# Further blocks' lists in the second pair, the first x copied in halves, and the second gather inside the first down product

## The reference

```python
logits = x @ w_router + b_router          # 320 x 32
top_v, top_i = lax.top_k(logits, 4);  top_w = softmax(top_v)
# rows of x are grouped by expert in blocks, and for every block:
g = jnp.minimum(xb @ w_gate[e] + b_gate[e], 7.0)
u = jnp.clip(xb @ w_up[e] + b_up[e], -7.0, 7.0)
y = (g * sigmoid(1.702 * g) * (u + 1.0)) @ w_down[e] + b_down[e]
# y rows times top_w are summed back into their tokens; gated residual, final RMSNorm
```

## Time and profile before

| | |
|---|---|
| median of three runs | 1199.6 us |
| the profiled execution's own time | 1199.98 us |
| its span in the trace | 1198.0 us (2 us lie around it) |
| TensorE (PE) matmul busy | 1145.7 us, 96% |
| VectorE (DVE), ScalarE (ACT) busy | 300.2 us, 153.6 us |
| moved by DMA | 452.67 MB, mean 378 GB/s |
| mean granted TensorE clock | 0.982 |
| pairs of experts | from 253 us to 1185 us |

### The profile page before, as it was taken

How to read it: one execution, slowest core, us unless ns; L and a number is a source line. 1 busy time by engine, 2 the same in 40 slices (tenths; PEclk the granted TensorE clock), 3 DMA queues, 4 the chain that set the end, 5 groups by cost and what they waited for, 6 DMA issues and landing times.

```text
span 1198.0 us, 15518 instructions
## 1 busy us (share of the span) xinstructions
PE 1145.7 (96%) x6469; PEld 534.2 (45%) x6470; DVE 300.2 (25%) x667; ACT 153.6 (13%) x257; POOL 38.7 (3%) x50
## 2 busy tenths in 40 slices
PE   5999999999999999999999999999999999999995
PEld 2666547554353525252535353535353434444332
DVE  3243423623121212020303030302031212121143
ACT  1342240311010000000000010101010101011002
POOL 1021200400000000000000000000000000000000
PEclk9889999999999999999999999999999999999998
DMA  9573567659999999999999999999999999999992
GB/s 381 224 271 132 207 265 336 228 212 428 382 429 421 427 426 427 426 428 426 427 428 428 428 427 429 427 427 428 429 428 429 429 428 428 429 429 419 429 421 89
DMA packets 38788, 452.67 MB, mean 378 GB/s; under 512 B 4176, under 2 KB 6608, under 8 KB 7632
## 3 DMA queue, kind: packets, MB, share of 16 engines
q1 hardware_dynamic: 37984, 449.31, 89.5%
q0 software_dynamic: 752, 2.60, 0.6%
HBM read 447.99 MB, written 3.91 MB: 377 GB/s over the span
## 4 chain that ended last, share of the span: by engine, by line
PE 75%; DMA 19%; DVE 3%; ACT 2%; issue 1%; SPq 0%; DVEq 0%
PE ps L618 74%; DMA arena<-in_w_exp 18%; DVE arena L1382 2%; ACT arena L1301 1%; DMA arena<-in_w_front 1%; DMA arena<-in_xT 1%; PE ps L996 0%; SPq L516 0%; DVE arena L1788 0%; PE ps L774 0%; DVE arena L1786 0%; DVE arena L1388 0%; DVE arena L1767 0%; PE ps L792 0%; ACT arena L1162 0%
## 5 line engine op out<-in xcount | busy, mean ns | idle before, releaser
L618 PE MATMUL ps<-arena 128*64 128x512 f32 (+9 forms) x6224 | 1116.9, 520 | 41.4 <-DMA arena<-in_w_exp 16.3
L618 PEld LDWEIGHTS ps<-arena 128*64 128x64 f32 (+4 forms) x6224 | 507.1, 147 | 642.1 <-issue 569.2
L1301 ACT ACTIVATE arena<-ps 128x1024 f32<-128x1024 f32 x46 | 45.5, 1022 | 527.5 <-PE ps L618 527.5
L1382 DVE TENSOR_TENSOR arena<-arena 128x1024 f32<-128x1024 f32 (+11 forms) x91 | 72.6, 819 | 55.1 <-ACT arena L1309 16.8
L1724 DVE TENSOR_SCALAR arena<-ps 128x1024 f32<-128x1024 f32 x15 | 18.4, 1223 | 266.3 <-PE ps L618 266.3
L1382 DVE TENSOR_TENSOR arena<-arena,ps 128x320 f32<-128x320 f32 (+2 forms) x116 | 57.1, 495 | 69.1 <-PE ps L618 64.2
L1732 DVE TENSOR_SCALAR arena<-ps 128x1024 f32<-128x1024 f32 x15 | 18.4, 1225 | 185.8 <-PE ps L618 185.8
L1309 ACT ACTIVATE arena<-arena 128x1024 f32<-128x1024 f32 x16 | 16.9, 1057 | 244.5 <-DVE arena L1724 229.1
L1717 DVE COPY arena<-arena 128x64 f32 (+3 forms) x32 | 5.0, 193 | 124.9 <-PE ps L618 124.9
L1710 DVE TENSOR_SCALAR arena<-arena 128x64 f32<-128x64 f32 (+3 forms) x96 | 23.0, 304 | 0.1
L1382 DVE TENSOR_TENSOR arena<-ps,arena 128x64 f32<-128x64 f32 (+10 forms) x39 | 13.2, 355 | 38.2 <-PE ps L618 34.0
(11 more groups left out here) (145 smaller groups left out, 172.6 us busy)
## 6 DMA issues: line engine op xcount, KB each, us to landing
arena<-in_w_exp SPq DMA_DIRECT2D x180, 2048.0 KB, 22.5
arena<-in_w_front SPq DMA_DIRECT2D x38, 1024.0 KB, 9.2
arena<-in_w_exp SPq DMA_DIRECT2D x24, 1024.0 KB, 24.3
arena<-in_s0T SPq DMA_DIRECT2D x1, 2048.0 KB, 14.4
out_ssmsT<-arena POOLq DMA_DIRECT2D x4, 512.0 KB, 6.4
arena<-in_xT SPq DMA_DIRECT2D x1, 1280.0 KB, 6.1
out_yT<-arena SPq DMA_DIRECT2D x4, 320.0 KB, 3.3
arena<-in_vec SPq DMA_DIRECT2D x1, 898.0 KB, 19.2
```

Source lines behind the costliest of these rows:

```text
L618: return pe.matmul(o, l, r, start=start, stop=stop, skip_group_check=True)
L1301: A(moe[name].rearrange("p (a b) -> p a b", a=2), ps[:, bank:bank + 2, :], ACT.Copy).then_inc(done, 1)
L1382: return V.tensor_tensor(o, a, b, op)
```

## The change

Three edits, all about pairs 0 and 1.

- The first gather raises a semaphore after its first half (4 of 8 column blocks, bank 6). ScalarE copies that half while TensorE gathers the other, then the other half. The first gate product starts when the first half is copied, and waits for the second between its own halves.
- In pair 0, gather(1) no longer stands between the up product and the transposes, but between the halves of the down product (`gather_second`, with a wait for `selT_ready`, since both use bank 7). The wait for x of pair 1 goes from pair 0's end, and ScalarE copies that x after the activation and the selection.
- `further_blocks` moves from pair 0's down product to pair 1's, with a new wait for pair 0's combine results to be added (`comb_added >= 8`, bank 2). VectorE's `further_lists` moves to its second turn, and the wait for `more_read` to pair 2.

Semaphores are renamed: `up_half` becomes `half_mm`, `y_half` becomes `half_copied`, with counts one higher in the last pair.

```diff
@@ gather @@
+                    if isinstance(q, int) and q == 0 and k == KC // 2 - 1:
+                        last.then_inc(half_mm, 1)
@@ pair @@
-                pe.wait_ge(x_ready, q + 1)
+                if first:
+                    pe.wait_ge(half_copied, 1)
+                else:
+                    pe.wait_ge(x_ready, q + 1)
...
-                product(0, 0, X, loads[0:PER // 3], slots[0:PER // 3], w)
+                product(0, 0, X, loads[0:PER // 3], slots[0:PER // 3], w, (lambda: pe.wait_ge(x_ready, 1)) if first else None)
...
-                if isinstance(q, int) and q == 1:
+                if isinstance(q, int) and q == 2:
                     pe.wait_ge(more_read, 1)
...
-                if not serial:
+                if not serial and not first:
                     gather(q + 1)
                 pe.wait_ge(act_ready, q + 1)
                 turn_act()
-                if not serial:
+                if not serial and not first:
                     pe.wait_ge(x_ready, q + 2)
...
-                product(2, 4, A, loads[2 * PER // 3:PER], slots[2 * PER // 3:PER], w, further_blocks if first else None,
+                later_middle = gather_second if first else None
+                if isinstance(q, int) and q == 1:
+                    later_middle = further_blocks
+                product(2, 4, A, loads[2 * PER // 3:PER], slots[2 * PER // 3:PER], w, later_middle,
                         q=q if split else None)
+
+            def gather_second():
+                pe.wait_ge(selT_ready, 1)
+                gather(1)
@@ further_blocks @@
                 pe.wait_ge(oh_ready, 1)
+                pe.wait_ge(comb_added, KC)
@@ scalar: ahead of the loop, and act_turn @@
-            copy_x(0)
+            act.wait_ge(half_mm, 1)
+            A(moe["X"][:, 0:AW], ps[:, 6, :], ACT.Copy).then_inc(half_copied, 1)
+            act.wait_ge(x_mm, 1)
+            A(moe["X"][:, AW:D], ps[:, 7, :], ACT.Copy).then_inc(x_ready, 1)
...
-                        copy_x(q + 1)
+                        first = isinstance(q, int) and q == 0
+                        if not first:
+                            copy_x(q + 1)
                         copy_act(q)
                         copy_sel(q)
+                        if first:
+                            copy_x(q + 1)
                         copy_y(q)
@@ dve_turn @@
-                    if first:
+                    second = isinstance(q, int) and q == 1
+                    if second:
                         further_lists()
```

More of the change, by code:

```diff
@@ L464, in build @@
                              "comb_mm", "comb_added"))
-        up_half, act_half, a_tr_half, actT_half, down_half, y_half = (
-            sem(n) for n in ("up_half", "act_half", "a_tr_half", "actT_half", "down_half", "y_half"))
+        half_mm, act_half, a_tr_half, actT_half, down_half, half_copied = (
+            sem(n) for n in ("half_mm", "act_half", "a_tr_half", "actT_half", "down_half", "half_copied"))
         x2_ready, xs2_ready, f_sq, f_sums, part_ready, mean_mm, root_done, yfin = (
@@ L1039, in last_pair @@
                 pe.wait_ge(comb_added, q * KC)
-                product(1, 2, X, loads[third:2 * third], slots[third:2 * third], half_done=up_half, q=q)
+                product(1, 2, X, loads[third:2 * third], slots[third:2 * third], half_done=half_mm, q=q)
                 def turn_half(h):
@@ L1059, in last_pair @@
                     if m == 0:
-                        pe.wait_ge(y_half, 1)
+                        pe.wait_ge(half_copied, 2)
                     if m == KC // 2:
@@ L1346, in last_copies @@
                 act.wait_ge(down_half, 1)
-                A(moe["y"][:, 0:AW], ps[:, 4, :], ACT.Copy).then_inc(y_half, 1)
+                A(moe["y"][:, 0:AW], ps[:, 4, :], ACT.Copy).then_inc(half_copied, 1)
                 act.wait_ge(exp_used, q * PER + PER)
@@ L1759, in activate_last @@
                     if h == 0:
-                        dve.wait_ge(up_half, 1)
+                        dve.wait_ge(half_mm, 2)
                     else:
@@ L1897, in dve_turn @@
                     pick_bias(caps(q + 1), perm, lambda s: (q + 1) * 2 + s)
-                    if first:
+                    second = isinstance(q, int) and q == 1
+                    if second:
                         further_lists()
-                    assert step.n == (OWN + 2 if first else OWN)
-                    if first:
+                    assert step.n == (OWN + 2 if second else OWN)
+                    if second:
                         start = start + 2
```

## The result

The changed kernel takes 1201.96 us at the median of twelve runs (1200.34 to 1204.93), the kernel before, timed beside it, 1198.51 (1196.59 to 1202.09). The ratio is 1.0022, 95% interval 1.0013 to 1.0031: **slower by 2.6 us** (1.6 to 3.7), where 1198.0 was forecast and the range ended at 1201.4. The profiled execution took 1201.73 us with a span of 1199.4.

A forecast was written before the change was run, and what follows sets the result against it. Bound: the stream of loads, its start and its gaps in pairs 0 and 1. Slack limits the gain to 3.3 us, 1.6 with one clock fall: 1199.98 - 1.6 = 1198.4, 0.4 above the median, so 1198.0; range 1195.6 to 1201.4.

The forecast's parts named there:

- The bound: From the third pair on, a full stream of loads with a fixed tail; standstills in pairs 0 and 1 lose 3.3 us.
- The x in halves: Pair 0's gate product starts 1.1 us earlier, and the stream restarts 1.1 us earlier.
- The handover and the gather: Pair 0: down starts 2.9 us earlier after 2.5 us idle; the gather between down's halves costs 5.3 us.
- the issue of 313.9: Load issued as down's second half in pair 0 frees slots: -4.0 + 5.3 - 5.1 = -3.8 us, thus at 310.1.
- I take one fall as the likelier, two in three: Pair 0's new handover: one clock fall likelier, two in three; bounds 0 and two low stretches (3.4 us).
- one chance in two: Clock falls behind the further blocks in pair 1: one chance in two, 1.7 us for each fall.
- n = 3: Three clock falls in pairs 0 to 2; the sum for the time gives a gain of -1.8 us.
- The sum for pair 2's issue: TensorE behind the ramp: -0.4 us against before, plus 1.7 us per clock fall; the start itself 1.1 us earlier.
- The sum for the time: Stream's gain at the narrowest place, 2.9 + 0.4 - 1.7n: 3.3 us without falls, 1.6 with one, -0.1 with two.
- The named rival "slower": Two low stretches in the handover, another behind the further blocks; queue dry at 419.97's loads; 1201.4 to 1202, chance 0.09.
- the issue of 301.73: Load issued as down's first half in pair 0 frees slots: -1.1 - 2.9 = -4.0 us, to 297.7.
- the two gaps of pair 0: Stream's losses at 302.5 to 305 us (0.9 us) and 313 to 316.5 us (2.4 us), both to be gone.

The follow-up runs named there:

- e8: e4 with fourteen idle 128x256 matmuls (6.0 us) between the halves of pair 0's down product; 1200.71 us, -0.2 against before.
- e4: e2 with the further blocks and their lists in pair 4 instead of pair 1; 1195.83 us, -3.6 against before.
- e2: Changed kernel with gather(1) back between up and the transposes of pair 0, the other two edits kept; 1196.02 us, -3.2 against before.
- e1: Kernel before with only the first x copied in halves; 1199.20 us, -1.2 against before.
- e3: Changed kernel with five idle 128x256 matmuls (2.1 us) ahead of pair 0's wait for the activation; 1199.54 us, -0.2 against before.
- e9: Changed kernel with five idle matmuls in pair 0's handover and the further blocks and lists in pair 4; 1196.05 us, -3.6 against before.
- e5: Kernel before with only gather(1) moved between the halves of pair 0's down, ahead of the further blocks; 1205.68 us, +5.2 against before.
- e10: Changed kernel with 36 transposes of 128x128 in pair 0's handover ahead of the wait for the activation; 1201.15 us, one execution.
- e11: Changed kernel with 22 matmuls of 128x128 in pair 0's handover ahead of the wait for the activation; 1202.43 us, one execution.
- e12: Changed kernel with two matmuls of 128x256 (0.85 us) in pair 0's handover ahead of the wait for the activation; 1198.61 us, one execution.
- e6: Changed kernel with the further blocks and their lists in pair 4 instead of pair 1; 1199.07 us, -0.2 against before.

## Why the prediction was wrong

**The bound** was right. The stream of loads and its gaps in pairs 0 to 2 decide: the gaps give the time of all ten kernels (the table), 6.0 us of added work cost only part of their length (e8), and 6.9 us taken away were worth no more than the gaps they closed (e4 against e2).

**The x in halves** was right: 1.1 us expected, 1.2 measured (e1, interval -0.1 to 2.5), and the product starts without a break behind the gather.

**The handover and the gather** were right as work. The wait is 2.6 us. With the handover at full clock (e3) down starts 289.40 - 260.36 = 29.04 us behind the first issue, against 293.43 - 261.62 = 31.81 before: 2.8 us earlier, 2.9 were expected. The issues of down's halves are 310.07 - 297.50 = 12.57 us apart, 7.0 + 5.3 = 12.3 were reckoned. From these terms, the issue of 313.9 was to move by 1.1 - 3.8 = -2.7 us against the first issue, plus 1.7 for each fall in the handover; with two of them +0.7. It is at 310.07 - 257.45 = 52.62 against 52.26, that is +0.4.

**"I take one fall as the likelier, two in three"** is the step that failed, together with the "one chance in two" for the further blocks. The handover brought two stretches at 0.50 and the further blocks one, n = 3 where I forecast n = 1. The sum for pair 2's issue, 1.1 - 0.4 + 1.7n, gives +5.8 us at n = 3, and +5.7 was measured. The sum for the time, 3.3 - 1.7n, gives 1.8 us slower; 2.6 were measured (1.6 to 3.7). The named rival "slower", with its count of falls and its 1201.4 to 1202, is what happened. I had given it 0.09.

Its place was not right, and that the sum comes so near is in part luck. The two stretches in the handover took the whole of its gain: the issue of 301.73 was to come 2.9 us earlier against the first, and it comes at 297.50 - 257.45 = 40.05 us behind it, against 40.11. So the two gaps of pair 0, which were to be gone, are there with 3.7 us (3.1 before). The first of them would have stayed in any case with the issue where it was: e2 and e4 have theirs at 40.1 us too and lose 0.9 and 1.0 us there; only e3 and e9, at 37.35, lose 0.1 and 0.2. And the queue ran dry in pair 1 (2.9 us lost), ahead of pair 2 (0.6), which I had named as the narrowest place.

Two misreadings made the chance of the slower case so small. I took the 2.7 us wait ahead of the fall at 625.8 us for the pattern of the handover, with one low stretch, and let two stretches stand only as an outer bound. And I took the further blocks' fall for one chance in two of one stretch. Nine profiles have the further blocks in pair 0 or 1 (before, changed, e1, e2, e3, e5, e10, e11, e12); behind them the clock was low for 0 to 2 stretches, eleven in all, 1.2 on the mean and not 0.5. The kernel before had one such stretch, in pair 0, where the stream had gaps anyway.

**Where the expected gain went.** The two edits that stay are worth 3.2 us (e2), the gather's move costs 5.8 on top. By e3 and e6, 2.8 us of that are given back either by filling the handover or by taking the lists out of the ramp, and by both together 6.2 (e9). The loss was not one wait: the clock made TensorE late in pair 0, and pair 1's extra work found no slack left.

**What stays open.** Why two low stretches follow the handover in two profiles and one in e5 was not told apart. Nor does the length of a wait alone tell whether the clock falls: in the trace before it was 0.50 from 861.3 us, behind a wait of 2.02 us, and 1.00 behind waits of 2.03 us (at 977.5) and 2.06 us (at 564.9). That the falls of the handover are in the other executions too is borne out by their mean clocks: e6 and e9 differ only in the filled handover and have 0.981 and 0.984 at the mean of ten each, the changed kernel and e3 0.981 and 0.983 at the mean of twelve (the scatter allows 0.001 either way). By an estimate, 6.8 us at half clock in 1199 are worth 0.003.

The tail was not quite fixed. From the landing at 1036 us to the end of the span it took 161.9 us before and 163.2 after; the chain after passes through loads that landed at 1096.6 and 1136.1 us, where before none stood in it. In this pair of executions the way from the first issue to the end is 5.9 us longer (944.3 against 938.4), of which the gaps explain 3.5 and this 1.3; the rest is not placed. What moved the tail was not tried.

## What to carry to other kernels

When TensorE waits for another engine and some work that could stand anywhere fills the wait, that work may be worth more than its own length: here it held the clock. Moving its 5.3 us out freed only 2.8, since TensorE then stood idle for 2.6; it cost all 5.3 at the new place, and up to 6.8 us at half clock behind the wait. Price each wait of a few microseconds that an edit opens on TensorE with the low stretch behind it, and where loads are the bound, put one-off work (here the lists) not where it is ready but where the engine already waits for loads. In the changed kernel that alone gave back 2.8 us (e6); e4 does it too and beats both kernels (1195.8 us), though it is not told apart from e2. Before either, compare the issues and the gaps of the stream from its first issue and not from the start of the trace: the front alone moved by up to 5.9 us between executions.

## What the runs showed of the hardware that I had not expected

The fp32 transposes hold the clock as matmuls do (e10, one execution: 1.00 through 5.5 us of them).

The stream does not end at once. At its end before (first two rows) and after (last three) the busy share of the 16 DMA engines and the rate fall off over some 6 us:

```profile
1168.00:1170.00 2.00, 2.00 (x12) 0.89 (x13) 0.00 (x0) 0.60 (x1) 0.00 (x0) 1.00 0.72 299
1172.00:1174.00 2.00, 2.00 (x12) 0.64 (x10) 0.00 (x0) 0.00 (x0) 0.00 (x0) 1.00 0.30 127
```

```profile
1168.00:1170.00 2.00, 2.00 (x12) 0.71 (x8) 0.00 (x0) 0.00 (x0) 0.00 (x0) 1.00 0.59 246
1172.00:1174.00 2.00, 2.00 (x12) 0.62 (x10) 0.00 (x0) 0.00 (x0) 0.00 (x0) 1.00 0.07 29
1174.00:1176.00 2.00, 2.00 (x12) 0.67 (x10) 0.00 (x0) 0.00 (x0) 0.00 (x0) 1.00 0.03 12
```

From the mean share I infer that the engines do not finish together: 0.07 is about one engine in sixteen. In the profile after, the share falls earlier than before, but the last bytes come later. Which engine is the last, and why, was not looked at.
